# First norm and first projections of a two-layer block in one program block, values first, rotary halves exchanged by ScalarE

## The reference

```python
h = rmsnorm(x, norm1_w[l])                       # x: 512 x 1024
p = jnp.einsum('bsd,dn->bsn', h, w_in[l])        # w_in: 1024 x 9248
(qa, ka, va, qkv_g, z, ...) = jnp.split(p, split_at, axis=-1)   # qa, ka, va: 1024 columns each
qa = apply_rope(qa.reshape(b, s, DA_HEADS, 2, DA_DH), cos, sin)
ka = apply_rope(ka.reshape(b, s, DA_HEADS, 2, DA_DH), cos, sin)

def apply_rope(t, cos, sin):                     # the last axis has 64 elements
    half = t.shape[-1] // 2
    rot = jnp.concatenate([-t[..., half:], t[..., :half]], axis=-1)
    return t * cos + rot * sin
```

## Time and profile before

| | |
|---|---|
| median of 3 runs | 2566.94 us |
| the profiled execution | 2568.99 us, its span 2567.2 us |
| PE, PEld (weight loads), DVE, ACT, POOL busy | 90%, 46%, 34%, 21%, 6% |
| block 1, to the first projection | 0 to 29.06 us |
| rotary units | 29.06 to 157.96 us |
| value units | 157.96 to 213.06 us |
| attention's block begins | 214.22 us |

### The profile page before, as it was taken

One profiled execution on the slowest core, in us unless ns is written; L12 is line 12 of the kernel. 1 busy time (PEld: TensorE's weight loads), 2 busy tenths in 40 slices (PEclk: granted clock), 3 DMA queues, 4 the chain that ended last, 5 costly groups with the idle time before them and its releaser, 6 DMA issues. The chain is left out here.

```text
span 2567.2 us, 30502 instructions
## 1 busy us (share of the span) xinstructions
PE 2307.6 (90%) x12724; PEld 1180.9 (46%) x12724; DVE 880.3 (34%) x1550; ACT 540.9 (21%) x959; POOL 165.2 (6%) x166
## 2 busy tenths in 40 slices
PE   6999999979999989997998888989898877999877
PEld 3444554447777764453333333333333223574343
DVE  1215766645766731113011010101010114444672
ACT  2004656632322313010000000000000003223131
POOL 0000000023433310000000000000000000120000
PEclk9999999989999999998999999999999998999889
DMA  5211000010111015235999999999999982202010
GB/s 196 72 58 68 34 34 1 0 42 27 26 35 27 26 59 197 113 125 214 427 428 428 428 427 428 428 428 428 427 427 428 428 345 68 67 33 70 33 49 34
DMA packets 93404, 488.52 MB, mean 190 GB/s; under 512 B 10781, under 2 KB 37683, under 8 KB 68563
## 3 DMA queue, kind: packets, MB, share of 16 engines
q1 hardware_dynamic: 91920, 486.34, 46.6%
q10 hardware_dynamic: 1347, 0.22, 0.0%
HBM read 483.14 MB, written 3.41 MB: 190 GB/s over the span
## 5 line engine op out<-in xcount | busy, mean ns | idle before, releaser
L1467 PE MATMUL PS<-SL,R 128*64 128x512 f32 x1168 | 262.3, 598 | 40.0 <-DMA SL<-w_gate 20.5
L1467 PE MATMUL PS<-R 128*64 128x512 f32 x880 | 197.3, 596 | 27.1 <-DMA R<-w_up 15.2
L1467 PEld LDWEIGHTS PS<-SL,R 128*64 128x64 f32 x1168 | 81.2, 137 | 216.2 <-issue 146.4
L1919 PE MATMUL PS<-HT,SL 128*128 128x512 f32 x384 | 169.6, 597 | 2.2 <-PEq L1662 2.2
L1635 DVE TENSOR_TENSOR HT<-HT,PS 128x512 f32<-128x512 f32 x32 | 20.6, 684 | 367.8 <-PE PS L1467 367.8
L1487 PE MATMUL PS<-SL,HT 128*64 128x512 f32 x280 | 124.4, 594 | 14.9 <-ACT HT L1575 7.0
L1467 PEld LDWEIGHTS PS<-R 128*64 128x64 f32 x880 | 60.8, 137 | 158.3 <-issue 108.7
L1488 PE MATMUL PS<-SL,HT 128*64 128x512 f32 x280 | 124.9, 596 | 0.0
L630 PE MATMUL PS<-HT,SL 128*128 128x512 f32 x256 | 119.2, 620 | 0.8 <-PEq L420 0.8
L348 PE MATMUL PS<-HT,SL 128*128 128x512 f32 x256 | 115.7, 606 | 3.5 <-PEq L235 2.6
L1640 DVE COPY HT<-PS 64x512 f32<-64x512 f32 x16 | 10.9, 684 | 305.5 <-PE PS L1488 305.5
(11 more groups left out here) (371 smaller groups left out, 3585.9 us busy)
## 6 DMA issues: line engine op xcount, KB each, us to landing
SL<-w_up SPq DMA_DIRECT2D x38, 2048.0 KB, 28.0
SL<-w_gate SPq DMA_DIRECT2D x35, 2048.0 KB, 30.2
SL<-w_down SPq DMA_DIRECT2D x35, 2048.0 KB, 27.3
R<-w_gate SPq DMA_DIRECT2D x29, 2048.0 KB, 29.5
R<-w_down SPq DMA_DIRECT2D x29, 2048.0 KB, 27.2
R<-w_up SPq DMA_DIRECT2D x26, 2048.0 KB, 29.2
SL<-w_in SPq DMA_DIRECT2D x19, 2048.0 KB, 8.8
X<-w_in SPq DMA_DIRECT2D x16, 512.0 KB, 3.9
```

The costliest lines, as they stand in the source:

```text
L1467: m = pe.matmul(banks[n][half * CAP:(half + 1) * CAP, :], XC[x // 2 % 2][:, 2 * j + k, toks], w[:, k, (2 * half + n) * 512:(2 * half + n + ...
L1919: m = pe.matmul(bank_[:, :], slab(i % 2)[:, k, j * P:(j + 1) * P], hT[:, k, :], start=(k == 0), stop=(k == KD - 1))
```

## The change

- The two blocks become one.
- **Loads.** SP issues all: tile 0 of `x`, the identity alone, the norm's gain broadcast to 128 partitions (`nrow`), tile 1, the first value slab, tiles 2 and 3, slab 0, the rotary tables, the 15 small loads that ACT issued, slabs 1 and 2, the rest of `tab`. The slabs' order is now 4, 0, 1, 2, 3, 5, 6, 7.
- **Norm.** Each tile has its own chain: square, ln, exp on ACT, and on DVE one operation that multiplies by the reciprocal root and by the gain (`scale`). One table set of ACT is loaded at the start.
- **Transposition.** PE turns a tile of tokens (`turn(t)`, 8 transposes into two banks), ACT copies the lower half of the features to `hT` and DVE the upper (`low`, `high`).
- **Order on PE.** turn 0, turn 1, value unit 0, turn 2, value unit 1, turn 3, value units 2 and 3, the 16 rotary units, the last four value units. The two transposes of the rows come behind the ninth unit.
- **Rotation.** No product by a matrix: ACT copies `raw` to `turned` in four instructions of 32 partitions each, to the neighbouring 32 partitions. The sign is in the sine table. The slab's buffer is freed by the count of units done.

```diff
+    t[:, T_SIN:T_SIN + S] = np.sin(ang) * np.where(np.arange(P) % 64 < 32, -1.0, 1.0)[:, None]
...
+                tile(0)
+                sp.dma_start(ident, io["table"][:, T_ID:T_ID + P]).then_inc(ident_in, 16)
+                sp.dma_start(nrow, io["norm1_w"].to_broadcast([P, D])).then_inc(nrow_in, 16)
+                tile(1)
+                weights(0)
+                tile(2)
+                tile(3)
+                weights(1)
+                sp.dma_start(R[5][:, 0:2 * S], io["table"][:, T_COS:T_BUCKET]).then_inc(rope_in, 16)
...
+                weights(2)
+                weights(3)
+                sp.dma_start(tab[:, P:T_KEEP], io["table"][:, P:T_KEEP]).then_inc(tab_in, 16)
+                for i in range(4, 8):
+                    sp.wait_ge(proj_done, 4 * (i - 3))
+                    weights(i)
...
+            @block.tensor
+            def _(pe):
+                def turn(t):
+                    pe.wait_ge(tile_scaled, t + 1)
+                    if t >= 2:
+                        pe.wait_ge(hT_low, t - 1)
+                        pe.wait_ge(hT_high, t - 1)
+                    for k in range(KD):
+                        m = pe.transpose(PS[4 + 2 * (t % 2) + k // 4][:, k % 4 * P:(k % 4 + 1) * P], hn[:, t, k * P:(k + 1) * P], ident)
+                        if k % 4 == 3:
+                            m.then_inc(tile_turned, 1)
+
+                pe.wait_ge(ident_in, 16)
+                turn(0)
+                turn(1)
+                for n, (kind, i, u) in enumerate(UNITS1):
+                    if n >= 4:
+                        pe.wait_ge(proj_evac, n - 3)
+                    bank_ = PS[n % 4]
+                    pe.wait_ge(slab_in[n // 4 % 4], 16 * (n // 16 + 1))
...
+                    m.then_inc(proj_done, 1)
+                    if n < 2:
+                        turn(n + 2)
...
+            @block.scalar
+            def _(act):
+                a = A()
+                nc.scalar.preload_act_table_set("natural_log_exp_and_others")
...
+                for n, (kind, i, u) in enumerate(UNITS1):
+                    act.wait_ge(proj_done, n + 1)
+                    if kind == "v":
+                        a(nc.scalar.activation(va[:, u, i * 512:(i + 1) * 512], PS[n % 4][:, :], ACT.Copy), proj_evac)
+                        continue
+                    if u >= 2:
+                        act.wait_ge(rope_done, u - 1)
+                    a(nc.scalar.activation(raw[u % 2], PS[n % 4][:, :], ACT.Copy), proj_evac)
+                    for q in range(4):
+                        a(nc.scalar.activation(turned[u % 2][32 * q:32 * q + 32, :], raw[u % 2][32 * (q ^ 1):32 * (q ^ 1) + 32, :], ACT.Copy),
+                          raw_turned if q == 3 else None, q == 3)
...
+                    v(nc.vector.tensor_tensor(t1, raw[u % 2], cosT, ALU.mult))
+                    dve.wait_ge(raw_turned, u + 1)
+                    v(nc.vector.tensor_tensor(t2, turned[u % 2], sinT, ALU.mult))
```

More of the change, by code:

```diff
@@ L48 @@
 T_KEEP = T_IOTA + CAP
-T_ROT = T_KEEP
-T_COS = T_ROT + P
+T_COS = T_KEEP
 T_SIN = T_COS + S
@@ L237, in _, with tile, weights @@
             def _(sp):
-                for t in range(NT):
+                def tile(t):
                     sp.dma_start(x3[:, t, :], io["x"][0, t * P:(t + 1) * P, :]).then_inc(tile_in[t], 16)
[L240 to L248, removed]
+                def weights(i):
+                    g = SLABS1[i]
+                    load_slab(sp, i % 4, w_in[:, g * 512:(g + 1) * 512], 512)
+                tile(0)
[7 more added lines that the diff above has]
+                sp.dma_start(R[5][:, 0:2 * S], io["table"][:, T_COS:T_BUCKET]).then_inc(rope_in, 16)
                 conv_rows = io["conv_w"][0].rearrange("t (c p) -> (t c) p", p=P)
-                act.dma_start(rows[0:120, 0:P], conv_rows).then_inc(rows_in, 16)
+                sp.dma_start(rows[0:120, 0:P], conv_rows).then_inc(rows_in, 16)
                 at_row = 0
@@ L255, in _ @@
                     src = src.rearrange("l (k p) -> (l k) p", p=P)
-                    act.dma_start(rows[at_row:at_row + n, P:2 * P], src).then_inc(rows_in, 16)
+                    sp.dma_start(rows[at_row:at_row + n, P:2 * P], src).then_inc(rows_in, 16)
                     at_row += n
                 for i, name in enumerate(("lambda_q1", "lambda_k1", "lambda_q2", "lambda_k2")):
-                    act.dma_start(lamrow[:, i, :], io[name].to_broadcast([P, 64])).then_inc(bc_in, 16)
+                    sp.dma_start(lamrow[:, i, :], io[name].to_broadcast([P, 64])).then_inc(bc_in, 16)
                 for i, name in enumerate(("a_log_fwd", "a_log_bwd", "dt_bias_fwd", "dt_bias_bwd")):
[L261 to L277, removed]
+                    sp.dma_start(al[:, 8 * i:8 * i + 8], io[name].to_broadcast([P, 8])).then_inc(bc_in, 16)
+                weights(2)
[4 more added lines that the diff above has]
+                    weights(i)
             @block.gpsimd
@@ L287, in _, with scale, high @@
                 v = V()
[L288 to L291, removed]
+                def scale(t):
+                    dve.wait_ge(tile_rstd, t + 1)
+                    if t == 0:
+                        dve.wait_ge(nrow_in, 16)
+                    v(nc.vector.scalar_tensor_tensor(hn[:, t, :], x3[:, t, :], stat[:, 8 + t:9 + t], nrow, ALU.mult, ALU.mult),
+                      tile_scaled)
+                def high(t):
+                    dve.wait_ge(tile_turned, 2 * t + 2)
+                    v(nc.vector.tensor_copy(hT[:, 4:8, t * P:(t + 1) * P],
+                                            PS[5 + 2 * (t % 2)][:, :].rearrange("p (k s) -> p k s", k=4)), hT_high)
+                scale(0)
+                scale(1)
+                high(0)
+                scale(2)
+                high(1)
+                scale(3)
+                high(2)
+                high(3)
                 dve.wait_ge(bc_in, 16 * 8)
@@ L296, in _ @@
                     v(nc.vector.reduce_sum(lam[:, i:i + 1], lamrow[:, 2 * i, :], AX), lam_dot)
[L298 to L310, removed]
@@ L315, in build @@
[L315 to L322, removed]
```

140 lines of the change are left out of this document (62 added, 78 removed).

## The result

The changed kernel takes 2539.51 us, the median of 4 runs (2536.53 to 2541.91), against 2567.15 us for the kernel before measured beside it (2565.26 to 2570.39). The ratio of the runs is 0.989, with a 95% interval of 0.9873 to 0.9908: 28 us faster, between 24 and 33. The forecast was 2539.0 us. The profiled execution took 2536.53 us, its span 2534.7 us, 32.5 us less than the span before.

A forecast was written before the change was run, and what follows sets the result against it. PE was taken as the bound, after a start chained through all engines. After: 13.4 + 164.6 + 3.15 + 3.1 + 0.7 = 185.0 against 212.5; 27.5 plus 0.4 off the median 2566.94 gives 2539.0 us, range 2533.5 to 2546.7.

The forecast's parts named there:

- Rotations and slab waits: In PE's projection units: rotations and waits at slab ends lie fully on PE's path; removing them saves 15.7 us.
- Copies at 0.63 us: ACT's four copies per rotary unit: 0.63 us each regardless of partitions, so ACT needs 3.2 of a unit's 6.86 us.
- the slower rival: Rotary units: at 2.6 us a copy, ACT becomes the bound and 43.7 us are lost, giving 2582.7 us; chance 0.02.
- Begin at 13.4 us: Start of value unit 0: released by its slab's landing, begin moves from 29.06 to about 13.4 us.
- Turns 2 and 3: Between the first value units: 16 transposes at 0.19 us now lie on PE's path, adding 3.1 us.
- two transposes of the rows: On PE among the units: hidden before, now on its path, adding 0.7 us together.
- Low clock, 3.15 us: PE's first units: time lost to a low granted clock, kept at 3.15 us as before.
- Sum: End of the last value unit: 185.0 us after against 212.5 before, 27.5 less; 27.9 with 0.4 added.
- 0.4 us added for pauses around rotations: End of the last value unit: added to the gain for what the sum before lacked of the traced 213.06 us.
- The late begin: First value unit: its slab lands only at 21.1 us, cutting the gain to 20.2 us, 2546.7 in all; chance 0.07.
- The low clock: First four value units: clock stays low through all, costing 27.4 us instead of 3.15, 2563.3 in all; chance 0.03.
- Given back: Stages behind the projections: a later stage begins at a transfer that doesn't move, leaving about 2567 us; chance 0.02.

The follow-up runs named there:

- experiment 1: Kernel before with only the exchange of halves moved to ScalarE and slabs freed by the count of units: 2554.58 us, ratio 0.9942 to the kernel before.
- experiments 1, 2: The second of these: changed kernel with the product by the rotation matrix back on TensorE and ScalarE's four copies gone: 2552.22 us, ratio 0.994 to the kernel before.
- experiment 3: Changed kernel with each rotary unit's four copies of 32 partitions made three times over: 2550.73 us, one run.
- experiment 4: Changed kernel with each rotary unit's four copies of 32 partitions made four times over: 2592.04 us, one run.
- experiment 7: Changed kernel with six identity products on TensorE ahead of turn 0 and two between turns 0 and 1: attention begins at 184.54 us.
- experiment 5: Changed kernel with rotary units before all value units, slabs in order 0 to 7, all four turns ahead of the first unit: attention begins at 194.56 us.
- experiment 9: Changed kernel with 13 identity products ahead of turn 0, 10 ahead of turn 1, 5 ahead of value unit 0: first unit 7.13 us, attention begins at 183.74.
- experiment 12: The changed kernel run once more, unaltered: 2538.81 us, ratio 0.9885 to the kernel before.

## Why the prediction was right

- *What bounds.* PE's path was the bound of the whole stretch; both parts came off it in full (experiments 1, 2).
- *Rotations and slab waits, 15.7 us:* 15.7 in experiment 1, with its earlier begin, its shorter low clock and its new wait taken out. That the 0.17 us taken off the value units' 55.10 is a last product's passage is something no run shows. The rows of the timeline overlap by as much (13.88 + 8.68 = 22.56 us, where the next begins at 22.39), and the first five rotary units take 79.08 - 44.74 = 34.34 us, 6.87 each.
- *Copies at 0.63 us, whatever the partitions:* 0.627. Their cover was right too: experiments 3 and 4 gave PE's waits within about a microsecond of what was computed from banks and units, and the barrier's share (2.5 and 5.1 us) was missing. The price of the slower rival, 43.7 us, lacks it too: 49.7 in experiment 4.
- *Begin at 13.4 us:* 13.88 in one execution and 15.46 in another. The slab released it, by 0.2 us over turn 1. The sum took tile 1's chain to end at 12.6; it ended at 13.7. Two terms of it were small by about half a microsecond each: tile 1 landed at 8.5 instead of 7.8, and its turn took 1.97 us instead of 1.5. The broadcast of the gain held up the first scaling (7.24 us, where tile 0 alone would have allowed 6.1), which the sum had left out; this cost tile 1 nothing, because its scaling waited for its own root at 10.3 us.
- *Turns 2 and 3, 3.1 us:* 1.7. This was the worst of the added terms. I took 0.19 us a transpose from a row at the start of the program, recorded at a granted clock of 1.00. That is a mean of two speeds: by windows of 1 us, four or five transposes begin in each up to 25 us, and eight in the next. Behind a unit, PE turns at 0.11. The two transposes of the rows, also taken from the start, cost 0.36 instead of 0.7.
- *Low clock, 3.15 us:* 1.65 in this execution, 0.8 to 2.0 in the five with this start. Experiment 1, whose start is the old one, lost 1.8 where the kernel before lost 3.15, so that the 3.15 of one trace was no fixed price. What sets the length of the slow stretch was not shown; the turns ahead of the unit take 1.94 and 1.97 us in all five.
- *Sum:* 27.9 forecast for the begin of attention, 30.35 measured in this execution: the begin took 0.5 off the gain, and the three terms above added 1.4, 0.3 and 1.5, together 2.7 us against the 2.45 found. The 0.4 us added for pauses around rotations should not have been: the terms after, with their measured sizes, give 182.2 us for the end of the last value unit, which the trace has at 182.7, so that as much is lacking there. With 27.5 for the forecast the gain comes to 30.2. The medians differ by 27.6. Of the two, the begin of attention is the cleaner figure for the change; that the median of 2539.51 meets the 2539.0 forecast within half a microsecond is partly luck, as the terms above missed by 2.45 us together and the rest of the kernel varies by several.
- *Rivals.* The late begin occurs in part and by chance (15.46 here, 15.64 in experiment 3), never to 21.1. The low clock lasted for some 3 us of the first unit, up to about 17 us, not for four units; between the value units there was no pause, and the second took 7.03 us, the third and fourth 13.90 together. Where pauses did stand before units, some of these were slow again: in experiment 4 units behind waits of 3.9 to 4.7 us take 8.8 to 9.7 us, and experiment 7's first unit takes 8.79 us behind pauses of 1.10 to 1.80 us. Slower by copies: experiment 4 is that case made real, and it was slower than before. Given back: the stages behind took 2.2 us less, not more.

## What to carry to other kernels

When a first product waits for a chain over all the data, look for the one whose operand is only a part, and give the transfers in the order in which the products need them: here the order of the products was worth 9 to 11 us, and a megabyte more ahead of the first weights cost 3.5. Work of the matrix engine that only moves data (an exchange of partition groups) is worth moving to an engine that idles, if that engine's time for a unit stays below the matrix engine's, as ACT's 3.2 us of 6.86 did here; in experiment 3 banks and later light units covered most of an excess of 1.6 us a unit. And a duration read at the start of a program may not hold later: here eight transposes took 1.94 us there and 1.04 us behind the first unit, with a granted clock of 1.00 recorded for both.

## What the runs showed of the hardware that was not expected

- A recorded granted clock of 1.00 at the start of these programs did not mean full speed. In the changed kernel eight transposes took 1.94 us, and the weight loads of 512-wide MATMULs began 0.85 us apart (14.89 and 15.74 us), with 1.00 beside them; later in the same trace it was 1.04 us for eight and 0.43 us apart.
- Behind three pauses of 1.1 to 1.8 us with 1.1 to 1.5 us of work between them the clock was back at 0.50 (experiment 7). It was 0.50 too behind a single pause of 2.64 us that followed 6.15 us of transposes (the kernel before). Behind a single pause of 2.29 us that followed a unit of 8.79 us, in experiment 4, the next unit took 7.13 us, at 1.00.
- The pace rose with only transposes on PE: nothing else was there from 20.3 to 26.4 us in the kernel before, and from 25 us on eight began in a microsecond instead of four or five, with 1.00 recorded throughout.
- The broadcast of one row of 4 KB to 128 partitions landed 5.5 and 6.9 us after its issue in two executions of the same kernel, with the same loads around it, and 7.4 in experiment 5.
- Code that no experiment touched differed by 7.6 us between executions, mostly in two stages that run at a granted clock below 1.00 in part. From the changed kernel's first MATMUL of line 641 to that of line 930 it is 175.0 us there (mean clock 0.91) and 179.4 in experiment 9 (0.89); from line 1930 to line 2301 it is 357.9 in experiment 12 (0.95) and 361.6 in experiment 9 (0.94). A change of under 0.2% can't be judged by whole times here, but its place in the trace can be read to within one or two, by how the same kernel's two traces differ (1.6 us at the first unit, 0.7 at attention).
